# Who waits for the outputs, where expert 14's down product stands, the order of the last additions, and an early square-root table

## The reference, cut to what matters

```python
def hier_moe(x, norm_g, w_rg, w_re, w_gate, w_up, w_down):      # 16 experts, each row takes 2
    u = rms_norm(x, norm_g)
    ...                                                        # group, top 2 inside it, dense_w
    h = jax.nn.silu(jnp.einsum('ntd,edf->ntef', u, w_gate)) * jnp.einsum('ntd,edf->ntef', u, w_up)
    h = h * dense_w[..., None].astype(h.dtype)
    return jnp.einsum('ntef,efd->ntd', h, w_down)

hp = hp + hier_moe(hp, ...)     # prompt rows; y_prompt = hp[:, 16:] after layer 1
hs = hs + hier_moe(hs, ...)     # sample rows; y_sample = hs after layer 1
```

## Time and profile before

| what | value |
|---|---|
| median of three executions | 1466.12 us |
| the profiled execution's own time | 1469.82 us |
| its span, first to last instruction | 1468.0 us |
| mean granted clock of PE | 0.935 of full speed |
| PE busy | 1322.7 us, 90% |
| PEld, DVE, ACT, POOL busy | 69%, 36%, 21%, 11% |
| DMA | 437.13 MB, mean 298 GB/s |

### The profile page before, as it was taken

How to read it: one execution, slowest core, us unless ns; L and a number is a source line. 1 busy time by engine, 2 the same in 40 slices (tenths; PEclk the granted TensorE clock), 3 DMA queues, 4 the chain that set the end, 5 groups by cost and what they waited for, 6 DMA issues and landing times.

```text
span 1468.0 us, 37154 instructions
## 1 busy us (share of the span) xinstructions
PE 1322.7 (90%) x15844; PEld 1013.0 (69%) x15844; DVE 522.3 (36%) x1164; ACT 301.0 (21%) x716; POOL 167.1 (11%) x201
## 2 busy tenths in 40 slices
PE   6959999999688979998989898999996899999994
PEld 5859989998445756766665555665444799999981
DVE  3341000000275546464645765664024211000005
ACT  2110000101131222212133543434011010001110
POOL 3100000010201000111121111120000100000011
PEclk9859999999988999999999999899997799999997
DMA  9929999997996679797978996975173599999965
GB/s 303 357 61 368 391 392 398 393 391 311 379 333 226 200 256 356 263 366 242 367 247 274 300 314 219 341 247 209 72 272 136 197 386 384 395 396 395 391 221 164
DMA packets 147194, 437.13 MB, mean 298 GB/s; under 512 B 20695, under 2 KB 51288, under 8 KB 138239
## 3 DMA queue, kind: packets, MB, share of 16 engines
q1 hardware_dynamic: 99463, 367.64, 67.5%
q10 hardware_dynamic: 37296, 38.09, 7.8%
q0 software_dynamic: 10320, 29.79, 6.4%
HBM read 406.38 MB, written 29.44 MB: 297 GB/s over the span
## 4 chain that ended last, share of the span: by engine, by line
PE 65%; issue 12%; DVE 8%; DMA 6%; ACT 4%; SPq 2%; ACTq 1%; POOL 1%; DVEq 0%; POOLq 0%
PE PS L1044 12%; PE PS L1048 11%; PE PS L1293 9%; PE PS L1076 6%; PE PS L1081 5%; PE PS L1428 5%; PE PS L991 3%; PE PS L1334 2%; PE PS L1372 2%; PE PS L1392 2%; PE PS L1380 2%; DMA W<-in_cache_v 1%; DMA KV<-yd,SLi 1%; DMA out_k_prompt<-W 1%; PE PS L983 1%
## 5 line engine op out<-in xcount | busy, mean ns | idle before, releaser
L1048 PE MATMUL PS<-W,KV 128*32 128x128 f32 x3072 | 345.7, 275 | 0.0
L1044 PE MATMUL PS<-W,KV 128*32 128x384 f32 x3072 | 342.5, 491 | 3.2 <-DVE KV L1962 3.2
L1048 PEld LDWEIGHTS PS<-W,KV 128*32 128x32 f32 x3072 | 337.9, 111 | 2.2
L2133 DVE TENSOR_TENSOR KV<-KV,PS 128x384 f32<-128x384 f32 x32 | 17.7, 554 | 483.1 <-PE PS L1062 426.8
L1293 PE MATMUL PS<-W 128*128 128x256 f32 x768 | 185.4, 397 | 0.7 <-ACT KV L1691 0.7
L1293 PEld LDWEIGHTS PS<-W 128*128 128x128 f32 x768 | 149.3, 200 | 32.2 <-issue 9.6
L1076 PE MATMUL PS<-W,KV 128*32 128x384 f32 x1440 | 162.3, 488 | 0.0
L1081 PE MATMUL PS<-W,KV 128*32 128x256 f32 x960 | 162.1, 327 | 0.0
L1044 PEld LDWEIGHTS PS<-W,KV 128*32 128x32 f32 x3072 | 151.9, 110 | 4.6 <-DVE KV L1962 4.1
L2272 DVE STREAM_TRANSPOSE KV<-KV 128x1024 f32<-128x1024 f32 x128 | 154.7, 1225 | 0.0
L1081 PEld LDWEIGHTS PS<-W,KV 128*32 128x32 f32 x960 | 95.6, 109 | 14.0
(11 more groups left out here) (294 smaller groups left out, 1503.0 us busy)
## 6 DMA issues: line engine op xcount, KB each, us to landing
W<-in_w_gate SPq DMA_DIRECT2D x32, 2048.0 KB
W<-in_w_up SPq DMA_DIRECT2D x32, 2048.0 KB, 14.3
W<-in_w_down SPq DMA_DIRECT2D x32, 2048.0 KB, 12.7
KV<-in_cache_k SPq DMA_DIRECT2D x256, 256.0 KB, 5.4
W<-in_cache_v SPq DMA_DIRECT2D x128, 512.0 KB, 7.8
yd<-KV ACTq DMA_DIRECT2D x30, 288.0 KB, 7.4
W<-in_w_kvf SPq DMA_DIRECT2D x4, 2048.0 KB, 21.4
W<-in_w_kvf ACTq DMA_DIRECT2D x8, 1024.0 KB, 8.5
```

The source lines that it names most:

```text
L1044: pe.matmul(PS[32 * q:32 * q + 32, bank, 0:WIDE], x, w[:, k, 0:WIDE], start=(k == 0), stop=(k == KC - 1), tile_position=(0, 32 * q), skip_ ...
L1048: mm = pe.matmul(PS[CAP:P, bank, P * q:P * q + P], x, w[:, k, WIDE:FF], start=(k == 0 and q == 0), stop=(k == KC - 1), tile_position=(0, C ...
```

## The change

SP's program ends with the waits that POOL's ended with, and POOL's ends after `moe(1)`. In both layers the gate product of expert 15 is cut in two: chunks 0 and 1, then the whole down product of expert 14, then chunks 2 to 7; the semaphore `gate_done` is raised with the last chunk. In layer 1 DVE adds expert 15's part of the first tile before it combines the fifth, and the fifth tile's gathers use buffers 2 and 3 and wait for the second `combine` instead of the first; in layer 0 buffers and wait stay as they were. After `moe(0)` ACT takes a square root of one column of `sd` that nobody reads before it is written again.

```diff
@@ block.sync, end of the program
+            for x in (LAST - 1, LAST):
+                sp.wait_ge(sem(f"row_out{x % 2}"), 16 * rows_stored(x))
+            sp.wait_ge(sem("state_out"), 16 * (NB + 1))
+            sp.wait_ge(sem("out_done"), 16 * OUTS)
+            sp.nop()
@@ block.gpsimd, end of the program
-            for x in (LAST - 1, LAST):
-                pool.wait_ge(sem(f"row_out{x % 2}"), 16 * rows_stored(x))
-            pool.wait_ge(sem("state_out"), 16 * (NB + 1))
-            pool.wait_ge(sem("out_done"), 16 * OUTS)
-            pool.nop()
@@ shared, and results() on POOL
+        def picked_buffer(l, n, ch):
+            return 2 * n + ch if n < 4 else 2 * l + ch
...
-                            buf = (2 * n + ch) % 8
+                            buf = picked_buffer(l, n, ch)
                             if n == 4:
-                                pool.wait_ge(sem("summed"), 1 + l * NT)
+                                pool.wait_ge(sem("summed"), 1 + l + l * NT)
@@ moe(l) on PE
-                def product(bank, slot, count, name):
+                def product(bank, slot, count, name, part=range(KC)):
...
-                    for k in range(KC):
+                    for k in part:
...
-                    mm.then_inc(sem(f"{name}_done"), 1)
+                    if KC - 1 in part:
+                        mm.then_inc(sem(f"{name}_done"), 1)
...
-                halves(NE - 1, 1, 0)
+                halves(NE - 1, 1, 0, range(0, 2))
                 down(NE - 2, 0)
+                halves(NE - 1, 1, 0, range(2, KC))
                 halves(NE - 1, 1, 1)
@@ ACT, after moe(0)
+            act.activation(sd[:, 0:1], sd[:, 0:1], ACT.Sqrt)
@@ DVE, moe(l) and the end of the program
                 if l == 1:
-                    for n in range(NT):
+                    for n in range(NT - 1):
                         combine(1, n)
...
             for n in range(NT):
+                if n == 1:
+                    combine(1, NT - 1)
                 last_added(1, n, 2 * n % 8)
```

More of the change, by code:

```diff
@@ L1084, in down, with halves @@
                     mm.then_inc(sem("down_done"), 1)
-                def halves(e, j, which):
+                def halves(e, j, which, part=range(KC)):
                     count = 8 * e + 16 - 8 * j
@@ L1091, in halves @@
                         after(pe, sem("silu_done"), e + l * NE)
-                        product(2, 3 * j, count, "gate")
+                        product(2, 3 * j, count, "gate", part)
                     else:
@@ L2189, in combine @@
                 for ch in range(2):
-                    ins = dve.scalar_tensor_tensor(out=H[0:r, t, :], in0=K8[0:r, (2 * n + ch) % 8, :], scalar=gm[0:r, ch, t:t + 1],
+                    ins = dve.scalar_tensor_tensor(out=H[0:r, t, :], in0=K8[0:r, picked_buffer(l, n, ch), :], scalar=gm[0:r, ch, t:t + 1],
                                                    in1=H[0:r, t, :], op0=ALU.mult, op1=ALU.add)
```

## The result

| | before | changed |
|---|---|---|
| median | 1468.05 us (14 runs, 1460.63 to 1478.22) | 1457.82 us (14 runs, 1453.83 to 1461.72) |
| ratio, 95% interval | | 0.9933 (0.9917 to 0.9950) |
| profiled execution, span | 1469.82, 1468.0 us | 1461.27, 1459.5 us |
| mean granted clock | 0.935 | 0.934 |
| PE busy | 1322.7 us, 90% | 1335.5 us, 92% |

The change is faster by 9.8 us (0.67% of 1468.05, from the ratio; the interval makes it 7.3 to 12.2); 1450 was forecast, a gain of 16.6. The time lies inside the range, but over a third of the forecast gain is missing. PE does the same 15844 instructions and is busy for 13 us longer. One of the six executions of the kernel without the split (second experiment) took 4147 us; its ratio is made without that one.

A forecast was written before the change was run, and what follows sets the result against it. PE's work bounds most of the span; the change touches each layer's expert end and the program's close. Layer 0's 4.2 plus layer 1's 12.4 make 16.6 us: profiled 1469.82 to 1453.2, 1450 on the median's basis, range 1442 to 1460.

The forecast's parts named there:

- Part 1: Program close: SP instead of POOL waits for the outputs, taking POOL's DRAIN off the path; gain 8.8 us, bounds 0 and 8.9.
- Rival (b): Program close: POOL's DRAIN waits for something the outputs or DVE's last reads settle and stays last; 7.9 us gain, 1458.2, chance 0.10.
- The cover: Program close: POOL's DRAIN would end at 1447 or 1453, ahead of the outputs' new end at about 1455.
- Part 4: Layer 0's end: square-root table loaded early, so the root starts at 401.60 instead of 402.72; gain 1.1 us, bounds 0 and 1.3.
- Part 2 in layer 0: Layer 0's last experts: expert 14's down product starts at 365.4 instead of 368.50; gain 3.1 us, bounds 0 and 3.1.
- rival (c): Layer 0's end: PE's shorter idle time keeps its clock up for 32 matmuls; some 3 us more, 1447, chance 0.07.
- Rival (a): Behind layer 0: its gain is swallowed by DMA load or waits elsewhere; 12.4 us remain, 1453.7, chance 0.20.
- Part 2 in layer 1: Layer 1's last experts: expert 14's down product and the gathers come 3.2 us earlier; a 0.6 us PE stall stays hidden.
- Rival (d): PE's stall at 1412.4 and its twin at 364.7: clock falls to 1.2 GHz, kernel slower at 1480, chance 0.03.
- Part 3: Layer 1's last additions: the first addition moves ahead of the second combine, so DVE's stall for tile 4's sums goes; 0.4 us.
- 2 us of stall: Layer 1's end: upper bound for DVE's wait before combining, if tile 4's gathers land late; nothing was taken.
- five terms of the sum: Gains forecast: layer 0's end 3.1 and 1.1 us; layer 1's end 3.2, 0.4 and 8.8 us; together 16.6 us.

The follow-up runs named there:

- the first experiment: The kernel before with only the closing waits and the nop moved from POOL to SP: 1455.82 against 1466.46 us, ratio 0.993.

## Why the prediction was right or wrong

**Part 1, SyncE waits: right.** The empty time went from 12.3 to 3.7 us; 8.8 forecast, 8.6 in the trace and 10.3 (7.5 to 13.1) in the experiment. The last instruction comes 0.5 us behind the last landing (1458.92), as forecast. Rival (b), a DRAIN that waits for the outputs, falls: the DRAIN ends at 1450.3, with four of DVE's five additions and all outputs but the first still to come. It ends 8.73 us behind the end of the last gather's issue (1440.54 + 1.00 in the trace), the same 8.73 as in the earlier trace rows. The cover was reckoned well, but it ends later than the forecast's 1447, because the fifth tile's gathers were late.

**Part 4, the table: right.** Nothing stands between DVE's mean square and the root (ACT's timeline, layer 0's end):

```profile
395.81 1.28 ACT L1663 ACT_TABLE_LOAD   x1
397.10 0.20 ACT L1663 ACTIVATE sd<-sd 128x1 f32<-128x1 f32 x1
400.78 1.06 ACT L1669 ACTIVATE KV<-H 64x1024 f32<-64x1024 f32 x1 [3.47 <-DVE H L2209]
...
402.14 0.20 ACT L1675 ACTIVATE sd<-ms 64x1 f32<-64x1 f32 x1 [0.21 <-DVE ms L1945]
```

From the start of the squares to that of the root it is 1.36 us against 2.46 in the kernel with wait and order alone: 1.1 us, as forecast. The Trainium skill's 2.66 us for a switch ("ScalarE: Activation LUTs", section "What ACT_TABLE_LOAD costs") has its first half confirmed, a load of 1.28; the root at 397.10 stands right behind it, with no drain of 1.38 between. By the estimate from that page this part would have been 2.5 us, and the measurement says 1.1.

**Part 2 in layer 0: right.** The down product starts 2.06 us behind the gate against 5.19, a gain of 3.13 (3.1 forecast), with a stall of 0.54. The gain passes through: PE restarts 36.5 us behind the gate (403.37 - 366.85) against 40.6 (403.95 - 363.31), 4.1 us earlier where 4.2 was forecast, and the store kept about its time (6.59 us against 7.42) as assumed. Of rival (c) a little is there too: PE's idle time before its restart fell from 9.28 to 2.38 us, the clock in 400 to 420 is 0.83 instead of 0.69, and the 32 matmuls take 8.41 us instead of 9.46. The idle time is shorter than the 4.5 us reckoned because layer 0 has some of layer 1's trouble: the clock falls to 0.50 in 386 to 388 us, `down_last` takes 8.80 us, and the sums start 28.6 us behind the gate instead of 25.8. The first addition there does not wait for them. Rival (a) is not borne out: from gate to gate the eight profiles with split and early root average 1039.5 us (1034.9 to 1043.8), the three with neither 1044.6 (1041.3 to 1047.8). The 5.1 us between the means are about the gain of 4.2, but the two groups overlap.

**Part 2 in layer 1: the step that failed.** The prediction asked whether "the store start[s] the gathers 3.2 us sooner", looked for what competes with the store, and said "so yes". They do start sooner, by 2.8 us (the stall was 0.81, not 0.6). What was not asked is what the gathers themselves do to PE, which then has expert 15's up product, a dense stream of narrow matmuls, some 20 records a microsecond, still to run. The shift of expert 15's work was put at 0.6 us and called hidden behind 5.5 us of cover. It was:

- 0.8 us for the stall,
- 7.6 us for the starved up product (L2140 follows its end, 24.4 us behind the gate; 16.0 + 0.8 would have been 16.8),
- 3.0 us for `down_last`, 10.1 instead of 7.1 at a granted clock of 0.50 to 0.91.

Together 11.4, and the first tile's sums do come at 37.2 instead of 25.8 us behind the gate. The first addition should have started at 32.7 (the fourth tile's combine at 33.4 - 3.2 = 30.2, and 2.5 us) and started at 39.2. These 6.5 us are the missing gain: 16.6 - 6.5 = 10.1, against 9.8 measured. Leaving out layer 1's split or making the up product's instructions few takes the loss away, and holding back the gathers takes most of it away, as the experiments show.

**Rival (d), slower by the clock: wrong in its place.** It had the clock fall on the stall at 1412.4. The clock stays at 1.00 through that stall and up to 1433. It does fall to 1.2 GHz, but behind some nine microseconds of starved work, a stretch for which the prediction had no rival.

**Part 3, the last additions: mis-sized.** 0.4 us forecast, 2.4 measured without the split. The bound of "2 us of stall" was on the wrong side. The 2.73 us wait for the fourth tile was read as one that "shrinks if they are out of its way", and then given no price. In the changed kernel this gain is buried under the wait for the sums.

So four of the five terms of the sum were good to about 2 us, and the fifth, layer 1's 3.2 us, came out 6.5 us worse and with the other sign. That 1457.8 lies inside the range, and next to rival (b)'s 1458.2, is luck as far as layer 1 goes: the range was not made wide for this loss, and rival (b)'s mechanism did not occur.

## What to carry to other kernels

When a product is moved forward, follow what it releases, and look at what each engine is doing when that arrives: here the gain in start was real, and the released gathers ran into the only engine that still had work. The same edit was worth 3 us in one layer and cost some 5 to 7 in the other, because in layer 0 the store takes longer and the gathers (15.7 us behind the gate) meet an up product that is nearly done. Let the engine with nothing slow to close wait for the outputs; this was worth over half a per cent for five moved lines.

## What the runs showed of the hardware

- POOL's indirect gathers, issued back to back 1.25 us apart, starve a dense stream of narrow matmuls: from 80 in 4 us to 16 and 12, from about 3 us behind the first issue on, in bursts mostly 1.4 us apart. With 64-byte rows at 8 GB/s it is the same (23 and 9); 16 wide matmuls take their usual 7.1 us. Bulk loads that SyncE issues don't do it: before, in 1414 to 1418, PE does 75 matmuls beside a DMA share of 1.00.
- The semaphore of the last narrow matmul can be late too: 2.4 us behind the matmul's end with the cut behind chunk 5, where no matmul was slow, and 3.9 us in the changed kernel's second profile, against 0.1 us in the kernel before. (The profile models the ends of matmuls.)
- By what path the gathers hold PE up stays open. It is neither bytes nor a releaser that the profile knows. That wide matmuls are spared points to the number of instructions, and the late semaphores point beyond the supply of them; no run here separates the two. The DMA packets that the profile calls "instruction" show nothing late: in the changed kernel one of 16 KB takes 0.92 us at 1420.3, and the next comes at 1436.5, behind the slow stretch.
- POOL's closing DRAIN ends 8.73 us behind the end of the issue of its last indirect DMA (8.73 to 8.75 in the nine other profiles with the new order of additions), with outputs still to come. Begun 20 us behind the last gather, in the kernel before, it takes the same 8.73 us. Only in the first experiment it ended 11.3 us behind (1444.7 against 1433.4); no run here shows why.
- The part between the two gates varies from one execution to the next: 1047.8 and 1041.3 us in the kernel before and in the one with SyncE's wait alone, which are the same program there. A gain of 4 us in that part has to be read from distances within a layer.
